# Every fourth late expert row of the prompt is weighted and summed by GpSimd instead of VectorE

## The chip, the cores and the metric

The kernel runs on one core of a Trainium2 chip. The metric is the device time of one execution in microseconds. Three runs of the kernel before took 5117.41, 5132.25 and 5138.71 us; their median, 5132.25 us, is the time before.

## The reference

One inference step of a two-layer backbone over 128 prompt tokens and 512 latent tokens, D = 1024, all in float32. Each layer has four token mixers whose results are merged through gates, an output projection, and then an expert layer. Only the expert layer matters here:

```python
def chunk(hc):                                     # 128 tokens
    qry = (hc @ w_query).reshape(-1, PEER_HEADS, 2, PEER_DK // 2)
    s = jnp.einsum('thpk,hpnk->thpn', qry, sub_keys)
    s1, i1 = lax.top_k(s[:, :, 0], PEER_TOPK)
    s2, i2 = lax.top_k(s[:, :, 1], PEER_TOPK)
    cand = (s1[..., :, None] + s2[..., None, :]).reshape(-1, PEER_HEADS, PEER_TOPK * PEER_TOPK)
    sc, ci = lax.top_k(cand, PEER_TOPK)
    e = ...                                        # 8 heads x 16 experts for each token
    g = jax.nn.softmax(sc, axis=-1)
    act = jax.nn.gelu(jnp.einsum('thkd,td->thk', u_tab[e], hc), approximate=False)
    return jnp.einsum('thk,thkd->td', g * act, v_tab[e])
```

So each token has 128 experts, and each expert a row of 2048 numbers (u, then v): the dot product of u with the token's vector gives a weight, and the result is the weighted sum of the 128 rows v. The 128 prompt tokens lie on the 128 partitions, so "row i" below is the i-th expert of every prompt token at once: 128 x 8 KB, 1 MB.

## The kernel before

The program has five instruction streams written out by hand (SyncE, GpSimd, ScalarE, VectorE, TensorE) that are tied by semaphores. Nothing reorders them: each engine runs its stream in the order of the code.

SyncE streams the weights in chunks of 512 KB through a ring of six (`wring`). GpSimd gathers the expert rows with indirect DMAs. For the prompt that are 128 rows in each layer (`PAIRS`). The first 16 (`EARLY`) are gathered while the latent tokens' queries and keys are made (L630). The other 112 are gathered (L664) during the latent tokens' merge (32 steps), output projection (8 steps) and expert query (16 steps): three rows in each merge step, one in each output step, one in each of the first eight query steps. They go into a ring of four slots, `prow`, with `NP = 4`.

What is done with row i, engine by engine:

- GpSimd waits on `p_acc` until row i-4 has been added, which frees its slot, and issues the gather of row i (L664).
- VectorE waits for the row (`p_row`), forms its dot product (`prompt_dot`, L1397) and then adds the row *before* it, i-1, to the sum `yacc` (`prompt_add`, L1407), when its weight is there.
- ScalarE makes the weight from the dot product: Gelu (L844), then times the gate (L845), counted on `p_w`.

`prompt_rows` gives VectorE's order: dot(i), add(i-1), dot(i+1), add(i), and so on. In a merge step it stands behind the evacuation of the gate product (L1633) and the addition to the merged sum (L1636). TensorE's merge step has 8 products against the gate's weights (L2129) and 4 against the branch's (L2134), each recorded as two matmuls, and may be two steps ahead of L1633. ScalarE makes the step's sigmoid (L1006), then the weights of that step's rows.

After the last add (row 127, in query step 8) VectorE routes the first latent tokens (L1137 to L1200); then GpSimd begins the 512 gathers of the latent tokens (L681). Before the second of these it waits for the prompt's last add, and so does TensorE before it turns `yacc`. In layer 0 and 1 all of this is the same.

Of the kernel before, what the change touches and what calls it, by code (L numbers as in the profile page):

```python
# [9 lines left out]
ALU = mybir.AluOpType  # L10
# [5 lines left out]
D = 1024  # L16
# [19 lines left out]
PAIRS = HEADS * TOPK  # L36
# [197 lines left out]
NP = 4  # L234
EARLY = 16
# [15 lines left out]
    return range(120 + n, 121 + n) if n < 8 else ()  # L251


class Chain:

    def __init__(self, eng, sem):
# [15 lines left out]
def need(eng, s, n):  # L272

    if n > 0:
        eng.wait_ge(s, n)


def backbone(nc, xT, cT, w, ada, small, rowg, lamrow, clay, poolw, subk, rope, edge, mask, bias, ckn, ckd,
             cvn, cvd, experts, y_prompt, y_sample, o_nk, o_nv, o_dk, o_dv):
    with ExitStack() as cx:  # L280
# [3 lines left out]
        def sem(name):  # L284
            return cx.enter_context(nc.semaphore(name))
# [6 lines left out]
        arena = sb("arena", [P, 28800])  # L292
# [24 lines left out]
        def at(tensor, start, *shape):  # L317
            n = int(np.prod(shape))
            v = tensor[:, start:start + n]
            if len(shape) == 1:  # L320
                return v
            names = "abcd"[:len(shape)]
            return v.rearrange(f"p ({' '.join(names)}) -> p {' '.join(names)}", **dict(zip(names, shape)))
# [68 lines left out]

        prow = [at(arena, a, 2 * D) for a in (16512, 18560, 10368, 14464)]
        prow0 = [at(arena, a, 2 * D) for a in (20096, 22144, 24704)]
        yacc0, yacc = at(arena, 27392, D), at(arena, 22656, D)
        pdots, pgel, pwcol = at(T, 2048, PAIRS), at(T, 2176, PAIRS), at(T, 2304, PAIRS)

        w_load = [sem(f"w_load{i}") for i in range(RING)]
# [15 lines left out]
        p_idx, p_top, p_gexp, p_gok = sem("p_idx"), sem("p_top"), sem("p_gexp"), sem("p_gok")  # L414
        p_row = [sem(f"p_row{i}") for i in range(NP)]
        p_row0 = [sem(f"p_row0{i}") for i in range(3)]
        p_dot, p_w, p_acc = sem("p_dot"), sem("p_w"), sem("p_acc")

        x_ready, sq_ready, root, h_ready = sem("x_ready"), sem("sq_ready"), sem("root"), sem("h_ready")
        sq_half = sem("sq_half")  # L420
# [56 lines left out]
        def row_of(i):  # L477
            return prow0[i % 3] if i < EARLY else prow[i % NP]

        def weight_of(i):  # L480
            return stp[:, i:i + 1] if i < EARLY else pwcol[:, i:i + 1]
# [4 lines left out]
        def pause(eng):  # L486

            eng.nop(nofuse=True)
# [34 lines left out]
        def _(gp):  # L523
            own = Chain(gp, pool_own)
# [76 lines left out]
            for l in range(DEPTH):  # L601
# [23 lines left out]
                gp.wait_ge(p_idx, 2 * l + 1)  # L625
                for i in range(EARLY):
                    if i >= 3:
                        gp.wait_ge(p_acc, l * PAIRS + i - 2)
                    pause(gp)
                    gp.indirect_dma_start(row_of(i), None, experts,  # L630
                                          bass.IndirectOffsetOnAxis(ap=peidx[:, i:i + 1], axis=0)).then_inc(p_row0[i % 3], 16)
                gp.wait_ge(p_acc, l * PAIRS + EARLY)
                pause(gp)
                vg = vscr.rearrange("(r c) n -> r c n", c=GRID_W)
                for j in range(NJ):
# [17 lines left out]

                gp.wait_ge(o_ready, NJOBS * (l + 1))
                gp.wait_ge(p_idx, 2 * (l + 1))
                for i in range(EARLY, PAIRS):
                    if i >= EARLY + NP:
                        gp.wait_ge(p_acc, l * PAIRS + i - NP + 1)
                    if i == EARLY + 3:
                        gp.wait_ge(y_diff, 4 * (l + 1))  # L660
                    if i == EARLY + 8:
                        pause(gp)
                        gp.dma_start(sk, subk[l]).then_inc(subk_in, 16)
                    gp.indirect_dma_start(row_of(i), None, experts,  # L664
                                          bass.IndirectOffsetOnAxis(ap=peidx[:, i:i + 1], axis=0)).then_inc(p_row[i % NP], 16)

                mixer = prompt_mixer(l + 1) if l + 1 < DEPTH else iter(())
                step = None
                for t in range(NL):
                    for i in range(PAIRS):  # L670
                        n = (l * NL + t) * PAIRS + i
                        here = t * PAIRS + i
                        if i % GP == 0:
                            gp.wait_ge(idx_ready, (l * NL + t) * 2 + i // GP + 1)
                        if here == 1:
                            gp.wait_ge(p_acc, PAIRS * (l + 1))
                        if here == 7:
                            wait_unit(gp, ("E", l, "ynP"))
                        if n >= NS:
                            gp.wait_ge(v_done, n - NS + 1)  # L680
                        gp.indirect_dma_start(rows[:, n % NS, :], None, experts,  # L681
                                              bass.IndirectOffsetOnAxis(ap=eidx[:, t % 2, i:i + 1], axis=0)).then_inc(row_in[n % NS], 16)
                        if here == PAIRS:
                            wait_unit(gp, ("C", l, "s15"))
                            step = next(mixer, None)
                        elif step is not None and here >= gather_of(step) + 10:
                            step = next(mixer, None)
# [423 lines left out]
        def _(v):  # L1111
            own = Chain(v, dve_own)
# [260 lines left out]
            def prompt_route(l):  # L1373

                for k in range(12, 16):
                    wait_freed(v, ("P", l, f"s{k}"))
                for g in range(2):
                    yield from route(l, proute, pscores[:, 8 * g:8 * g + 8, :], peidx[:, GP * g:GP * (g + 1)], pgate[:, GP * g:GP * (g + 1)],
                                     p_idx, p_top, lambda: need(v, p_acc, l * PAIRS))

            def prompt_soften(l):

# [16 lines left out]
            def prompt_add(l, i):  # L1399

                v.wait_ge(p_w, l * PAIRS + i + 1)
                row = row_of(i)[:, D:2 * D]
                if i == 0:
                    v.tensor_scalar(yacc0, row, weight_of(i), None, ALU.mult).then_inc(p_acc, 1)
                else:
                    v.wait_ge(p_acc, l * PAIRS + i)
                    v.scalar_tensor_tensor(yacc0 if i < EARLY else yacc, row, weight_of(i), yacc0 if i <= EARLY else yacc, ALU.mult, ALU.add).then_inc(p_acc, 1)  # L1407

            def prompt_rows(l, which):

                for i in which:
                    prompt_dot(l, i)
                    if i not in (0, EARLY):
                        prompt_add(l, i - 1)

            mixer = prompt_mixer(0)
# [8 lines left out]
            for l in range(DEPTH):  # L1425
# [285 lines left out]
                for n in range(17):  # L1711
                    if n < 16:
                        prompt_rows(l, prompt_rows_at("query", n))
                    if n >= 1:
                        take_scores("L", 0, n - 1)
                    if n == 8:
                        prompt_add(l, PAIRS - 1)
                        for k in range(4, 8):
                            wait_freed(v, u(f"s{k}"))
                        first = latent_route(0, 0)  # L1720
                    if first:
                        for _ in range(10):
                            next(first, None)
# [43 lines left out]
        def _(pe):  # L1767
# [195 lines left out]
            for l in range(DEPTH):  # L1963
# [228 lines left out]

                for t in range(2):
                    turn_norm(t)
                pe.wait_ge(p_acc, PAIRS * (l + 1))
                turned(("E", l, "ynP"), [yacc[:, k * P:(k + 1) * P] for k in range(KD)])

                def turn_experts(t):
# [146 lines left out]
```

## Time and profile before

| | |
|---|---|
| three runs | 5117.41, 5132.25, 5138.71 us |
| the profiled execution | 5121.45 us |
| its span, first to last instruction | 5119.6 us |
| granted TensorE clock, mean | 0.966 |
| merge, output and query stage with the late prompt rows, layer 0 | 861.9 to 1343.7 us |
| the same, layer 1 | 3307 to 3787 us |

The profile is one execution. Busy time is the time in which an engine works on its instructions; GpSimd's time for a gather is that of issuing it, not of the transfer. Idle time is put down to what ended it. "Issue to landing" runs from the start of the issuing instruction until the data has arrived.

### The profile page before, as it was taken

What the parts mean: (1) busy time and instruction counts of PE and PEld (TensorE: products, weight loads), DVE (VectorE), ACT (ScalarE), POOL (GpSimd) and SP (SyncE); (2) the same over time, 40 slices, a digit from 0 to 9 for tenths busy, and PEclk for the clock granted to TensorE, in tenths of its full rate; (3) what the DMA queues carried; (4) which work ended last, traced back from release to release, by engine and by line L of the source; (5) the groups of instructions that cost most, each with busy time, mean ns of one, the idle gap of its engine ahead of it and who ended that gap; (6) DMA issues with size and microseconds to landing.
All of it is one profiled execution on the core that took longest, in us unless ns stands there. A gap on an engine that the chain in (4) does not pass through costs nothing.

```text
span 5119.6 us, 46892 instructions
## 1 busy us (share of the span) xinstructions
PE 4417.8 (86%) x14388; PEld 2284.2 (45%) x14388; DVE 3388.3 (66%) x7266; ACT 1951.3 (38%) x5074; POOL 1661.8 (32%) x1600
## 2 busy tenths in 40 slices
PE   7889888998899888888888898999889987777777
PEld 4674455434645333344544444644464632222222
DVE  4239865777787677775444896777778767576544
ACT  1210543343233434565533035544323433333333
POOL 3003121223244453433332322132224444434332
PEclk8899989999999999999999998999999999999999
DMA  7752526999799999999999143199979999999998
GB/s 286 252 192 79 191 78 249 350 345 351 305 420 420 420 420 411 413 394 418 405 419 419 60 140 124 61 356 356 360 279 420 412 419 422 422 421 419 421 421 353
DMA packets 277115, 1677.27 MB, mean 328 GB/s; under 512 B 31808, under 2 KB 31856, under 8 KB 112384
## 3 DMA queue, kind: packets, MB, share of 16 engines
q0 software_dynamic: 190896, 1365.43, 66.0%
q1 hardware_dynamic: 82944, 302.03, 16.1%
q10 hardware_dynamic: 3024, 6.82, 0.3%
q8 instruction: 115, 1.88, 0.1%
q14 instruction: 136, 1.11, 0.1%
HBM read 1667.33 MB, written 6.82 MB: 327 GB/s over the span
## 4 chain that ended last, share of the span: by engine, by line
DMA 39%; PE 31%; DVE 17%; ACT 7%; issue 5%; POOL 0%; SPq 0%; DVEq 0%; ACTq 0%; POOLq 0%
DMA arena<-experts,bsb 27%; PE ps L2218 12%; DMA arena<-experts,peidx 10%; PE ps L1805 5%; DVE arena L1496 4%; DVE arena L1708 3%; PE ps L1913 2%; PE ps L1980 2%; DMA wring<-w 2%; DVE arena L1407 2%; PE ps L2070 2%; PE ps L2092 2%; PE ps L1781 1%; ACT L1066 1%; ACT T L1070 1%
## 5 line engine op out<-in xcount | busy, mean ns | idle before, releaser
L2218 PE MATMUL ps<-arena,T 128*128 128x512 f32 x4096 | 1967.6, 614 | 445.2 <-ACT T L1070 444.6
L1708 DVE CUSTOM_DVE_ANT_0 arena<-arena,h_sb 128x1024 f32<-128x1024 f32 x1024 | 1252.8, 1227 | 865.0 <-DMA arena<-experts,bsb 861.4
L681 POOL DMA_INDIRECT arena<-experts,bsb x1024 | 1095.8, 1070 | 1741.4 <-PE ps L2218 1582.2
L2218 PEld LDWEIGHTS ps<-arena,T 128*128 128x128 f32 x4096 | 726.1, 192 | 1569.5 <-ACT T L1070 951.7
L1066 ACT ACTIVATE bsb<-T 128x1 f32<-128x1 f32 x1024 | 205.9, 201 | 1303.0 <-DVE T L1708 1301.3
L1805 PE MATMUL ps<-h_sb,wring 128*128 128x256 f32 (+2 forms) x2304 | 517.8, 382 | 35.1 <-DVE h_sb L1447 13.7
L2129 PE MATMUL ps<-h_sb,wring 128*128 128x512 f32 x1024 | 457.6, 600 | 33.5 <-DVE arena L1633 31.0
L1805 PEld LDWEIGHTS ps<-h_sb,wring 128*128 128x128 f32 x2304 | 380.7, 196 | 183.8 <-issue 152.0
L664 POOL DMA_INDIRECT arena<-experts,peidx x224 | 249.5, 1114 | 655.6 <-DVE arena L1407 582.1
L1070 ACT ACTIVATE T<-ident,bsb 128x128 f32<-128x128 f32 x1024 | 410.9, 401 | 33.5
L1397 DVE CUSTOM_DVE_ANT_0 arena<-arena,h_sb 128x1024 f32<-128x1024 f32 x256 | 312.7, 1222 | 113.7 <-DMA arena<-experts,peidx 112.6
L1980 PE MATMUL ps<-wring,h_sb 128*128 128x512 f32 x768 | 338.2, 598 | 0.0
L2129 PEld LDWEIGHTS ps<-h_sb,wring 128*128 128x128 f32 x1024 | 192.6, 191 | 294.3 <-issue 228.1
L1067 ACT ACTIVATE bsb<-bsb,T 128x1 f32<-128x1 f32 x1024 | 301.4, 294 | 33.2
L1407 DVE SCALAR_TENSOR_TENSOR arena<-arena,T 128x1024 f32<-128x1024 f32 x224 | 287.0, 1281 | 0.5 <-ACT T L845 0.5
L2134 PE MATMUL ps<-arena,wring 128*128 128x512 f32 x512 | 230.2, 593 | 0.0
L1980 PEld LDWEIGHTS ps<-wring,h_sb 128*128 128x128 f32 x768 | 146.2, 193 | 175.3 <-issue 175.3
L844 ACT ACTIVATE T<-T 128x1 f32<-128x1 f32 x224 | 45.3, 202 | 444.0 <-DVE T L1397 444.0
L1496 DVE SCALAR_TENSOR_TENSOR arena<-arena,sm 128x512 f32<-128x512 f32 x240 | 184.9, 849 | 0.0
L1805 PE MATMUL ps<-arena,wring 128*128 128x256 f32 (+1 forms) x768 | 150.4, 353 | 25.8 <-DVEq L1639 25.0
L2070 PE MATMUL ps<-arena 64*128 64x128 f32 (+2 forms) x512 | 151.8, 433 | 17.3 <-ACT T L961 15.2
L630 POOL DMA_INDIRECT arena<-experts,peidx x32 | 64.9, 2029 | 284.4 <-DVE arena L1407 171.6
(326 smaller groups left out, 4543.1 us busy)
## 6 DMA issues: line engine op xcount, KB each, us to landing
wring<-w SPq DMA_DIRECT2D x576, 512.0 KB, 6.2
arena<-experts,bsb POOLq DMA_INDIRECT x1024, 15.3
bsb<-bias POOLq DMA_DIRECT2D x16, 512.0 KB, 3.8
arena<-subk POOLq DMA_DIRECT2D x4, 1024.0 KB, 8.3
arena<-experts,peidx POOLq DMA_INDIRECT x256, 8.0
arena<-v_scratch POOLq DMA_DIRECT2D x64, 64.0 KB, 2.0
x_sb<-xT POOLq DMA_DIRECT2D x1, 2048.0 KB, 14.1
v_scratch<-arena ACTq DMA_DIRECT2D x8, 256.0 KB, 2.0
```

Source lines behind the costliest of these rows:

```text
L681: gp.indirect_dma_start(rows[:, n % NS, :], None, experts, bass.IndirectOffsetOnAxis(ap=eidx[:, t % 2, i:i + 1], axis=0)).then_inc(row_in[ ...
L1066: own.link(act.activation(gel[:, i:i + 1], dots[:, t % 2, i:i + 1], ACT.Gelu))
L1067: own.link(act.activation(wcol[:, i:i + 1], gel[:, i:i + 1], ACT.Copy, scale=gate[:, t % 2, i:i + 1]))
L1070: act.activation(diag[:, n % ND, :], ident[:], ACT.Copy, scale=wcol[:, i:i + 1]).then_inc(diag_ok, 1)
L1397: v.tensor_tensor_reduce(e, e, htok(NL), 1.0, 0.0, ALU.mult, ALU.add, d).then_inc(p_dot, 1)
L1407: v.scalar_tensor_tensor(yacc0 if i < EARLY else yacc, row, weight_of(i), yacc0 if i <= EARLY else yacc, ALU.mult, ALU.add).then_inc(p_acc, 1)
L1496: op = v.scalar_tensor_tensor(acc[:, c, :], U[:, c, 1 + k:1 + k + LAT], S(col), acc[:, c, :], ALU.mult, ALU.add)
L1708: v.tensor_tensor_reduce(e, e, htok(t), 1.0, 0.0, ALU.mult, ALU.add, dots[:, t % 2, i:i + 1]).then_inc(dot, 1)
L1805: mm = pe.matmul(bank(key, cols), chunk_of(s, l, c)[:, k * P:(k + 1) * P], src(k), start=(k == 0), stop=(k == KD - 1))
L1980: mm = pe.matmul(bank(key), h_sb[:, t, k, :], chunk_of("L", l, c0 + q)[:, kk * 512:(kk + 1) * 512], start=(k == 0), stop=(k == KD - 1))
L2129: mm = pe.matmul(ps[:, s % 2, :], chunk_of("L", l, c)[:, k * P:(k + 1) * P], h_in(k), start=(k == 0), stop=(k == KD - 1))
L2218: mm = pe.matmul(ps[:, 6 + half, :], diag[:, n % ND, :], rows[:, n % NS, D + half * 512:D + (half + 1) * 512], start=(i == 0), stop=(i == ...
```

## The change

Of the rows from 16 on, those with i % 4 == 2 (18, 22, ..., 126; 28 of 112) are no longer added by VectorE. GpSimd sums them into a second accumulator `yaccg`. It does so in its own stream, just before the gather that reuses the slot: wait for the row's weight, multiply the row in place by its weight, add it to `yaccg`, wait for its own completion, then issue the gather. For row 18 the multiply writes `yaccg` directly. After the loop it sums row 126. VectorE, after adding row 127, adds `yaccg` to `yacc`. Since `p_acc` now counts only what VectorE adds, `added(l, i)` gives the counts to wait for, 101 in a layer instead of 128.

```diff
+def pool_row(i):
+    return i >= EARLY and i % NP == 2
+
+POOL_ROWS = sum(pool_row(i) for i in range(PAIRS))
+ADDED = PAIRS - POOL_ROWS + 1
+
+def added(l, i):
+    return l * ADDED + sum(not pool_row(j) for j in range(i + 1))
...
-        yacc0, yacc = at(arena, 27392, D), at(arena, 22656, D)
+        yacc0, yacc, yaccg = at(arena, 27392, D), at(arena, 22656, D), at(arena, 23680, D)
...
@@ gpsimd
+                def prompt_sum(i):
+                    k = l * POOL_ROWS + (i - EARLY) // NP
+                    gp.wait_ge(p_w, l * PAIRS + i + 1)
+                    pause(gp)
+                    row = row_of(i)[:, D:2 * D]
+                    if i < EARLY + NP:
+                        gp.tensor_scalar(yaccg, row, weight_of(i), None, ALU.mult).then_inc(p_accg, 1)
+                    else:
+                        own.link(gp.tensor_scalar(row, row, weight_of(i), None, ALU.mult))
+                        gp.tensor_tensor(yaccg, yaccg, row, ALU.add).then_inc(p_accg, 1)
+                    gp.wait_ge(p_accg, k + 1)
+                    pause(gp)
+
                 for i in range(EARLY, PAIRS):
                     if i >= EARLY + NP:
-                        gp.wait_ge(p_acc, l * PAIRS + i - NP + 1)
+                        if pool_row(i - NP):
+                            prompt_sum(i - NP)
+                        else:
+                            gp.wait_ge(p_acc, added(l, i - NP))
...
+                prompt_sum(PAIRS - 2)
...
                         if here == 1:
-                            gp.wait_ge(p_acc, PAIRS * (l + 1))
+                            gp.wait_ge(p_acc, ADDED * (l + 1))
...
@@ vector
-                                     p_idx, p_top, lambda: need(v, p_acc, l * PAIRS))
+                                     p_idx, p_top, lambda: need(v, p_w, l * PAIRS))
...
             def prompt_rows(l, which):
                 for i in which:
                     prompt_dot(l, i)
-                    if i not in (0, EARLY):
+                    if i not in (0, EARLY) and not pool_row(i - 1):
                         prompt_add(l, i - 1)
...
                         prompt_add(l, PAIRS - 1)
+                        v.wait_ge(p_accg, POOL_ROWS * (l + 1))
+                        v.wait_ge(p_acc, added(l, PAIRS - 1))
+                        v.tensor_tensor(yacc, yacc, yaccg, ALU.add).then_inc(p_acc, 1)
...
@@ tensor
-                pe.wait_ge(p_acc, PAIRS * (l + 1))
+                pe.wait_ge(p_acc, ADDED * (l + 1))
```

GpSimd's stream in the prompt's late gathers of layer 0 before: all 112 gathers (L664) stand together, parted only by the load of `subk` (L663).

```order
L664 DMA arena<-experts,peidx 128x2048 x8
L663 DMA arena<-subk 128x2048
L664 DMA arena<-experts,peidx 128x2048 x104
L681 DMA arena<-experts,bsb 128x2048 x129
```

The same place now (L697 is the gather, L696 the load of `subk`, L679 and L681 the multiply, L682 the addition to `yaccg`):

```order
L697 DMA arena<-experts,peidx 128x2048 x6
L679 TENSOR_SCALAR arena<-arena,T 128x1024
L697 DMA arena<-experts,peidx 128x2048 x2
L696 DMA arena<-subk 128x2048
L697 DMA arena<-experts,peidx 128x2048 x2
L681 TENSOR_SCALAR arena<-arena,T 128x1024
L682 TENSOR_TENSOR arena<-arena 128x1024
L697 DMA arena<-experts,peidx 128x2048 x4
L681 TENSOR_SCALAR arena<-arena,T 128x1024
L682 TENSOR_TENSOR arena<-arena 128x1024
L697 DMA arena<-experts,peidx 128x2048 x4
```

The last four rows repeat. A multiply and an addition now stand between every fourth gather and the one behind it.

VectorE's stream in a merge step before (L1633 the evacuation, L1397 a dot product and the read of its sum, L1407 the add of the row before):

```order
L1633 TENSOR_TENSOR arena<-ps,arena 128x2x256
L1397 ISA arena,T<-arena,h_sb 128x1024
L1397 ISA T 128x1
L1407 SCALAR_TENSOR_TENSOR arena<-arena,T 128x1024
L1397 ISA arena,T<-arena,h_sb 128x1024
L1397 ISA T 128x1
L1407 SCALAR_TENSOR_TENSOR arena<-arena,T 128x1024
L1397 ISA arena,T<-arena,h_sb 128x1024
L1397 ISA T 128x1
L1407 SCALAR_TENSOR_TENSOR arena<-arena,T 128x1024
```

The same step now (L1667 is L1633, L1431 is L1397, L1441 is L1407):

```order
L1667 TENSOR_TENSOR arena<-ps,arena 128x2x256
L1431 ISA arena,T<-arena,h_sb 128x1024
L1431 ISA T 128x1
L1431 ISA arena,T<-arena,h_sb 128x1024
L1431 ISA T 128x1
L1441 SCALAR_TENSOR_TENSOR arena<-arena,T 128x1024
L1431 ISA arena,T<-arena,h_sb 128x1024
L1431 ISA T 128x1
L1441 SCALAR_TENSOR_TENSOR arena<-arena,T 128x1024
```

Here the add behind the first dot product, that of GpSimd's row, is gone. Every fourth add is gone so; everything else keeps its order.

## Rows read from the trace of the kernel before

**Rows 1.** The page's totals: engine, busy us, share of the span, instructions.

```profile
PE 4417.8 (86%) x14388; PEld 2284.2 (45%) x14388; DVE 3388.3 (66%) x7266; ACT 1951.3 (38%) x5074; POOL 1661.8 (32%) x1600
```

**Rows 2.** Chain of waits, 862 to 1330 us: shares by line, then start us, us, what.

```profile
by line: DMA arena<-experts,peidx 57.0%; issue 10.7%; PE ps L1805 10.0%; DVE arena L1407 8.8%; PE ps L2129 4.5%; PE ps L2134 2.2%; PE ps L2159 1.1%; DVE T L1397 0.6%; ACT L1006 0.5%; DVE arena L1397 0.5%; DVE T L1439 0.4%; DVE bsb L1166 0.4
861.88 7.11 PE ps L2129 x16
...
872.42 6.87 PE ps L2129 x16
...
1069.19 1.21 DVE arena L1407
1070.66 7.95 DMA arena<-experts,peidx
```

**Rows 3.** Merge stretches: length; PE, PEld, DVE, ACT, POOL busy; clock; DMA share; GB/s.

```profile
950.00:1030.00 80.00, 71.50 (x163) 30.41 (x162) 57.64 (x75) 32.80 (x62) 22.18 (x20) 1.00 0.92 347
1030.00:1110.00 80.00, 78.36 (x177) 33.54 (x176) 60.75 (x79) 33.64 (x65) 23.63 (x22) 0.98 0.93 351
```

**Rows 4.** Waits from 862 to 1330 us: total us, times, longest.

```profile
POOL arena L664 <- DVE arena L1407: 291.3, 107, 9.8
DVE arena L1397 <- DMA arena<-experts,peidx: 59.4, 55, 4.4
PEld ps L2129 <- DVE arena L1633: 37.2, 24, 4.0
```

**Rows 5.** The gathers L664 from 860 to 1300 us.

```profile
L664 POOL DMA_INDIRECT arena<-experts,peidx x109: 932/936/1953, 878.1 to 1293.5; - x109
DMA to landing us min/median/max: 5.5/8.2/11.0
```

**Rows 6.** Timeline of VectorE, then of ScalarE, in one merge step.

```profile
1067.96 1.23 DVE L1397 CUSTOM_DVE_ANT_0 arena<-arena,h_sb 128x1024 f32<-128x1024 f32 x1 [1.16 <-DMA arena<-experts,peidx]
1069.11 1.28 DVE L1407 SCALAR_TENSOR_TENSOR arena<-arena,T 128x1024 f32<-128x1024 f32 x1
1071.79 0.69 DVE L1633 TENSOR_TENSOR arena<-ps,arena 128x512 f32<-128x512 f32 x1 [1.40 <-ACT arena L1006]
...
1069.22 0.20 ACT L844 ACTIVATE T<-T 128x1 f32<-128x1 f32 x1 [3.06 <-DVE T L1397]
1069.46 0.30 ACT L845 ACTIVATE T<-T,pgate 128x1 f32<-128x1 f32 x1
```

**Rows 7.** GpSimd's own operations, by line and in the timeline.

```profile
L604 POOL TENSOR_TENSOR arena<-x_sb x8: 1882/1890/1912, 100.2 to 2833.1; 128x1024 f32<-128x1024 f32 x8
L560 POOL TENSOR_SCALAR arena<-arena x8: 527/664/932, 83.6 to 1883.3; 128x128 f32<-128x128 f32 x8
L560 POOL TENSOR_SCALAR bsb<-bsb x8: 1502/1734/1737, 425.6 to 2944.9; 128x512 f32<-128x512 f32 x8
...
85.48 0.29 POOL L588 COPY arena<-arena 128x128 f32<-128x128 f32 x1 [0.19 <-POOL arena L592]
...
423.58 0.61 POOL L617 COPY bsb<-arena 128x512 f32<-128x512 f32 x1 [52.60 <-ACT arena L870]
424.34 1.08 POOL L549 TENSOR_TENSOR bsb<-bsb 128x543 f32<-128x543 f32 x1 [0.15 <-POOL bsb L617]
```

**Rows 8.** VectorE and GpSimd at the same time: the convolution; later a dot product.

```profile
429.63 35.49 DVE L1496 SCALAR_TENSOR_TENSOR arena<-arena,sm 128x512 f32<-128x512 f32 x34
464.38 15.98 DVE L1496 SCALAR_TENSOR_TENSOR arena<-arena,sm 128x512 f32<-128x512 f32 x24
L1496 DVE SCALAR_TENSOR_TENSOR arena<-arena,sm x20: 737/1092/1780, 429.6 to 449.8; 128x512 f32<-128x512 f32 x20
...
1715.04 1.90 POOL L579 TENSOR_TENSOR arena<-x_sb 128x1024 f32<-128x1024 f32 x1
...
1714.51 3.52 DVE L1708 CUSTOM_DVE_ANT_0 arena<-arena,h_sb 128x1024 f32<-128x1024 f32 x1 [0.86 <-DMA arena<-experts,bsb]
```

**Rows 9.** GpSimd's first gather for the latent tokens in layer 0.

```profile
1343.74 0.94 POOL L681 DMA_INDIRECT arena<-experts,bsb  x1 [49.31 <-DVE bsb L1200]
```

More of the change, by code:

```diff
@@ L416, in backbone @@
         p_row0 = [sem(f"p_row0{i}") for i in range(3)]
-        p_dot, p_w, p_acc = sem("p_dot"), sem("p_w"), sem("p_acc")
+        p_dot, p_w, p_acc, p_accg = sem("p_dot"), sem("p_w"), sem("p_acc"), sem("p_accg")
         x_ready, sq_ready, root, h_ready = sem("x_ready"), sem("sq_ready"), sem("root"), sem("h_ready")
@@ L627, in _ @@
                     if i >= 3:
-                        gp.wait_ge(p_acc, l * PAIRS + i - 2)
+                        gp.wait_ge(p_acc, added(l, i - 3))
                     pause(gp)
@@ L631, in _ @@
                                           bass.IndirectOffsetOnAxis(ap=peidx[:, i:i + 1], axis=0)).then_inc(p_row0[i % 3], 16)
-                gp.wait_ge(p_acc, l * PAIRS + EARLY)
+                gp.wait_ge(p_acc, added(l, EARLY - 1))
                 pause(gp)
@@ L1405, in prompt_add @@
                 else:
-                    v.wait_ge(p_acc, l * PAIRS + i)
+                    v.wait_ge(p_acc, added(l, i - 1))
                     v.scalar_tensor_tensor(yacc0 if i < EARLY else yacc, row, weight_of(i), yacc0 if i <= EARLY else yacc, ALU.mult, ALU.add).then_inc(p_acc, 1)
```

## The prediction

> **What bounds the kernel now.** I began with the page's own totals. No engine fills the span: TensorE is busy 86% of it, VectorE 66%, GpSimd 32% [rows 1]. So what the change is worth has to be read in its own stage, the merge, output and query steps of the latent tokens, in which the 112 late prompt rows are gathered. In layer 0 that stage runs from 861.9 us to the first latent gather at 1343.7 us [rows 2, 9]; layer 1 repeats it.
>
> The chain of waits over that stage is the view that decides: 57% of it is a prompt row in flight from DRAM, 8.8% the VectorE add L1407, and TensorE's matmuls have only the smaller part [rows 2]. The reader should see there a regular alternation: a row's transfer of some 8 us, then the add of 1.21, then the next transfer. The stretches of 80 us say the same from the engines' side [rows 3]: TensorE is busy 72 to 79 of 80, VectorE 58 to 61, the DMA engines 0.92, but nothing is at its limit all the time.
>
> The waits name the loop [rows 4]. GpSimd stands idle 291 us in this stage of layer 0 until an add L1407 is done; VectorE stands idle 59 us until a row has landed; TensorE waits for the evacuation L1633, which is queued on VectorE behind those rows. In the code a slot of the four-row ring is free only when the row's add is done, and that add stands on VectorE behind the dot product of the *next* row. So one turn of the loop is: GpSimd issues row j+3, it lands, its dot product, the add of row j+2, the issue of row j+6. From the rows [rows 5, 6]: issue to landing 8.2 (median), dot product 1.14 from its start to the add's start, add 1.28, 0.27 from its end (1070.39) to the next issue (1070.66 [rows 2]): 10.9 us for three rows, 14.5 for four. Measured are 108 intervals of issues in 1293.5 - 878.1 = 415.4 us [rows 5], 3.85 us each, 15.4 us for four rows. The loop explains nearly all of the pace; the rest are turns in which VectorE waits for a gate (1.40 us in the timeline [rows 6]).
>
> **The change, part by part.** Counted from the code, for each layer: 28 rows (18, 22, ..., 126) leave VectorE. 28 scalar_tensor_tensor of 1.28 go, and one tensor_tensor of 128x1024 comes ahead of the latent routing (about 1.23). GpSimd gets 28 tensor_scalar and 27 tensor_tensor of 128x1024, in line with its own gathers.
>
> *What VectorE saves.* 1.28 us in four rows. VectorE is busy 60 us of 80 [rows 3], about 11.5 of the 15.4 us of four rows, and idles for the rest. By itself this gives nothing unless the freed 1.28 stood on the loop; on GpSimd's path it is replaced by something longer.
>
> *What GpSimd pays.* A tensor_tensor of this very size takes 1.89 [rows 7]. The tensor_scalar has no row of this size: the multiply by a constant on 512 elements takes at least 1.50 and on 128 at least 0.53 [rows 7], which is 2.54 ns for each further element, so 0.53 + 896 x 2.54 ns = 2.80 us. Between dependent GpSimd instructions lie 0.15 us [rows 7].
>
> *The shared read.* When GpSimd's pooling runs beside VectorE's convolution, both stretch. Thirty-four scalar_tensor_tensor take 35.49 us, where 24 of them without company take 15.98, 0.67 each [rows 8]; GpSimd's 512-element multiply goes from 1.50 to a median of 1.73 [rows 7]. One dot product, 1.23 otherwise [rows 6], takes 3.52 around a GpSimd tensor_tensor of 1.90 [rows 8]. I give each GpSimd operation 0.3 us of waiting. The dot product, scalar_tensor_tensor and tensor_tensor that fill this stage on VectorE all read two tensors of SBUF, so this will be met here. This is the rule of the Trainium skill, page "SBUF — State Buffer", section "Who interferes with whom": a VectorE instruction with two SBUF inputs and a GpSimd instruction that reads SBUF exclude each other, and the second waits for the whole first one. By that rule, the trace agrees, with the 3.52.
>
> On VectorE's side a pair can cost up to 3.52 - 1.23 = 2.3 us for the tensor_tensor and, from L1496's median of 1.09 against its least of 0.74 [rows 8], 0.35 on 512 elements, perhaps 0.7 for the multiply. That is 3.0 against 1.28 saved, so VectorE's load *rises* by up to 1.7 us in four rows, to 13.2 of 15.4. It stays covered by VectorE's idle time.
>
> *The new turn.* Let row p be one of GpSimd's. When VectorE has added row p-1, GpSimd issues row p+3 (0.27 + 0.94). Its weight is long there (two short instructions of ScalarE after the dot product, 0.20 and 0.30 [rows 6]). Then it multiplies (0.15 + 2.80 + 0.30), adds (0.15 + 1.89 + 0.30), goes on (0.15) and only now issues row p+4: 6.95 us after the add of p-1. Before, that issue waited for the add of row p, which could be done some 2.4 us (1.14 + 1.28) after the add of p-1. Row p+4 lands, its dot product takes 1.14, and behind it stands the add of row p+3 (1.28), which corresponds to the add of p-1: the turn of four rows is closed. Queued on GpSimd behind the pair are the gathers of p+4 and p+5, whose slots may already be free; on VectorE the dot products of those rows wait, behind them the evacuation L1633, and TensorE for that.
>
> The landing is the unknown. The median is 8.2 us with 0.92 of the DMA engines busy; the fastest landing took 5.5 [rows 5]. Row p+4 goes out after a pause of 5.7 us in which no row was issued, so it meets a link with less in it than the median row. I take 7.0, near the middle. The turn is then 6.95 + 7.0 + 1.14 + 1.28 = 16.4 us against 15.4: 1.0 us more. At 5.5 it would be 14.9, under the present pace, and no loss; at 8.2 it is 17.6, 2.2 more.
>
> *The sum.* 26 such turns in a layer (rows 22 to 122; row 18 has one operation and 126 no gather behind it) by two layers by 1.0 us = 52 us. The added tensor_tensor stands ahead of the routing on which the first latent gather waits, so it is fully on the path: 2 x 1.23 with its hand-over, 3 us. The routing's wait, moved from the adds to the weights, and the changed semaphore targets cost nothing: they are met long before. The latent expert stage behind it keeps its instructions. The profiled execution took 5121.45 us; 5121.45 + 55 = 5176. It lies 10.8 us under the median of the three runs (5132.25), from which the same sum gives 5187. I predict 5182.
>
> **The rivals.**
>
> *B, a cheap multiply: no change.* If GpSimd multiplies by a column at the pace at which it copies (0.29 for 128 elements, 0.61 for 512 [rows 7], so 0.61 + 512 x 0.83 ns = 1.04 us), the turn is 14.6 us at a landing of 7.0, below today's 15.4. The pair then hides in GpSimd's idle 291 us, and other turns of the loop set the pace as now: 5121.45 + 3 = 5125 us. Against it stands that the row of the tensor_scalar itself is three times as steep as that of the copy. For it, that this row multiplies by a constant and the new one by a column, which no row shows. The Trainium skill's page "GPSIMD Engine Reference", section "Engine selection", speaks for B: operations with one input run at roughly one element per cycle on GpSimd. By it the time would be B's, by the tensor_scalar's row the forecast's; the trace agrees for the copy, not for the tensor_scalar.
>
> *C, VectorE's relief counts: faster.* Place: TensorE waits for the evacuation L1633, 24 times and 37.2 us in this stage of layer 0 [rows 4]. In three steps of four an add of 1.20 would be gone from ahead of it: 24 x 3/4 x 1.2 = 21.6 us a layer, 43 in both, less the 3: 5081 us. It decides only if the GpSimd turn falls well below the present one, that is if the two operations with their gaps take under about 4 us, and if GpSimd's reads don't hold VectorE up, which rows 8 speak against. TensorE's own work of a step (872.42 - 861.88 = 10.5 us in the first, which waits for nothing [rows 2]) and the DMA engines at 0.92 leave little room below 11.
>
> *D, the slow end.* The landing stays at 8.2 because VectorE's dot products, stretched by the shared read, are late too: 52 x 2.2 + 3 = 117, 5239 us.
>
> **How the numbers follow.** The forecast has 0.60, B 0.24, C 0.06, D 0.10. A difference of 0.5%, 26 us on the median of 5132, is about what a measurement of this kernel can tell from none. The forecast and D lie above 5158, which gives slower 0.70; B, with a little of C, is "same", 0.25; the rest of C is faster, 0.05. The range takes in B's 5125 and ends at D's 5239: 5123 to 5240. What is left out is C and the tail above D. The forecast's own range is 5160 to 5220.
>
> **What would show it.** In the profile after: GpSimd's tensor_scalar of 128x1024 at 2.8 to 3.1 us and its tensor_tensor at 1.9 to 2.2, once in four gathers; four issues of rows in 16.4 us instead of 15.4; more idle time of VectorE until a row has landed, above 59 us a layer; dot products of more than 1.23 us where GpSimd reads; the first latent gather about 27 us later in each layer, and everything behind it as long as before. I am wrong if the multiply takes about 1 us (B), if rows issued behind the pair land in 5.5 us and the pace stays at 15.4, or if TensorE's waits for L1633 shrink.

## The result, and the profile after

The changed kernel takes 5221.24 us (median of 4 runs, 5216.61 to 5225.03) against 5135.14 for the kernel before: the ratio is 1.0177, 95% interval 1.0159 to 1.0194. It is 86 us slower. The forecast was 5182, with 5123 to 5240 as the range; the direction was right, and the size was underestimated: the sum had 55 us. The narrower range given for the forecast's own mechanism, 5160 to 5220, is missed by 1 us, and the time lies nearer to rival D's 5239 than to 5182.

The page's totals after, as in [rows 1]: span; then busy us, share and instructions of each engine.

```profile
span 5223.2 us, 47006 instructions
PE 4452.4 (85%) x14388; PEld 2295.9 (44%) x14388; DVE 3410.5 (65%) x7212; ACT 1952.7 (37%) x5074; POOL 2010.0 (38%) x1710
```

VectorE has 54 instructions fewer and is busy 22 us *longer*. GpSimd is busy 348 us more. The span has grown by 103.6 us from one profiled execution to the other; the medians differ by 86, since the execution profiled before was one of the quick ones (5121.45) and the one after, 5225.03, wasn't.

Where the time went: GpSimd's first latent gather of layer 0, the end of the stage [rows 9].

```profile
1396.24 1.01 POOL L715 DMA_INDIRECT arena<-experts,bsb  x1 [34.71 <-DVE bsb L1234]
```

It is 52.5 us later than before, where the prediction had about 27, and layer 1 repeats it: its first latent gather comes at 3890.3 instead of 3787.3, 103.0 later. From there to the last gather layer 1 takes 1302.7 us, before 1303.0: the rest has not changed.

The new operations (name: least, median, most ns):

```profile
L681 POOL TENSOR_SCALAR arena<-arena,T x54: 2859/2860/3742, 906.7 to 3848.7; 128x1024 f32<-128x1024 f32 x54
L682 POOL TENSOR_TENSOR arena<-arena x54: 2337/2347/3420, 909.6 to 3852.0; 128x1024 f32<-128x1024 f32 x54
```

The multiply is where its own row of before put it (2.80 and 0.3), not where the copy's row would have (1.04): rival B is gone. The addition takes at least 2.34, not the 1.89 of [rows 7]. That row multiplies a tensor by itself, the new one adds two tensors; which of the two differences counts, no run shows.

Waits from 862 to 1375 us, as in [rows 4]:

```profile
POOL arena L697 <- DVE arena L1441: 149.9, 61, 7.3
DVE arena L1431 <- DMA arena<-experts,peidx: 92.0, 49, 5.3
PEld ps L2166 <- DVE arena L1667: 57.2, 17, 5.5
...
POOL arena L697 <- POOL arena L682: 20.5, 26, 0.9
```

GpSimd waits less for adds (149.9 instead of 291.3), since it works in that time. VectorE waits more for rows (92.0 instead of 59.4), and TensorE more for the evacuation (57.2 instead of 37.2). The last row is new: after each pair GpSimd stands still for 0.79 us before the gather. (Pair beside, below, shows that 0.5 of it is the `pause` of the kernel.)

Two stretches of the merge, as in [rows 3]:

```profile
950.00:1030.00 80.00, 69.69 (x157) 29.70 (x156) 55.13 (x63) 31.39 (x57) 50.56 (x30) 0.98 0.87 326
1030.00:1110.00 80.00, 69.35 (x150) 29.64 (x149) 53.05 (x63) 28.97 (x56) 47.91 (x28) 0.94 0.81 295
```

The DMA engines are less busy (0.81 to 0.87, before 0.92 to 0.93): there are holes in the stream of rows. TensorE is less busy too, and its granted clock is lower, 0.98 and 0.94 after 1.00 and 0.98 in the same stretches. Its products against the gate's weights take 626 ns in the mean of both layers instead of 600. Whether this slower clock is part of the cause is taken up with the turn, below.

One turn of the ring, first GpSimd, then VectorE (start us, us, what, idle before and its releaser):

```profile
1073.93 1.79 POOL L697 DMA_INDIRECT arena<-experts,peidx  x1 [0.66 <-DVE arena L1441]
1075.76 2.86 POOL L681 TENSOR_SCALAR arena<-arena,T 128x1024 f32<-128x1024 f32 x1
1078.70 2.83 POOL L682 TENSOR_TENSOR arena<-arena 128x1024 f32<-128x1024 f32 x1
1082.31 1.19 POOL L697 DMA_INDIRECT arena<-experts,peidx  x1 [0.78 <-POOL arena L682]
1083.80 1.99 POOL L697 DMA_INDIRECT arena<-experts,peidx  x1 [0.30 <-issue]
...
1092.99 0.94 POOL L697 DMA_INDIRECT arena<-experts,peidx  x1 [5.95 <-DVE arena L1441]
...
1078.11 1.22 DVE L1431 CUSTOM_DVE_ANT_0 arena<-arena,h_sb 128x1024 f32<-128x1024 f32 x1
1079.25 3.37 DVE L1441 SCALAR_TENSOR_TENSOR arena<-arena,T 128x1024 f32<-128x1024 f32 x1
1082.54 1.21 DVE L1431 CUSTOM_DVE_ANT_0 arena<-arena,h_sb 128x1024 f32<-128x1024 f32 x1
...
1090.29 1.23 DVE L1431 CUSTOM_DVE_ANT_0 arena<-arena,h_sb 128x1024 f32<-128x1024 f32 x1 [5.33 <-DMA arena<-experts,peidx]
1091.44 1.28 DVE L1441 SCALAR_TENSOR_TENSOR arena<-arena,T 128x1024 f32<-128x1024 f32 x1
```

Follow the loop: issue of row p+3 at 1073.93; pair; issue of p+4 at 1082.31; its dot product at 1090.29, for which VectorE had waited 5.33 us; the add of p+3 behind it at 1091.44; the issue of p+7 at 1092.99. This turn took 19.1 us, 2 more than the mean. Beside it stands the second effect: the add at 1079.25 lasts 3.37 instead of 1.28. It begins while GpSimd's addition runs (1078.70 to 1081.53) and ends 1.1 us behind it. The gathers behind the pair take 1.19 and 1.99 to issue instead of 0.94.

### The profile page after: what moved, and what is told of

Read it like the earlier page. It is cut to its first block, busy times and chain, and to the rows that moved or that the text cites. A ratio compares the mean times of both kernels' runs of the same rounds, so it can differ in the third digit from the quotient of the medians.

```text
span 5223.2 us, 47006 instructions
## 1 busy us (share of the span) xinstructions
PE 4452.4 (85%) x14388; PEld 2295.9 (44%) x14388; DVE 3410.5 (65%) x7212; ACT 1952.7 (37%) x5074; POOL 2010.0 (38%) x1710
## 4 chain that ended last, share of the span: by engine, by line
DMA 35%; PE 30%; DVE 17%; ACT 8%; issue 7%; POOL 4%; SPq 0%; DVEq 0%; ACTq 0%; POOLq 0%
DMA arena<-experts,bsb 26%; PE ps L2255 12%; DMA arena<-experts,peidx 6%; PE ps L1842 5%; DVE arena L1530 4%; DVE arena L1742 3%; PE ps L1950 2%; PE ps L2017 2%; DMA wring<-w 2%; PE ps L2107 2%; PE ps L2129 2%; POOL arena L697 2%; DVE arena L1441 1%; ACT L1100 1%; ACT T L1104 1%
## 5 line engine op out<-in xcount | busy, mean ns | idle before, releaser
L1742 DVE CUSTOM_DVE_ANT_0 arena<-arena,h_sb 128x1024 f32<-128x1024 f32 x1024 | 1252.9, 1227 | 867.4 <-DMA arena<-experts,bsb 860.9
L715 POOL DMA_INDIRECT arena<-experts,bsb x1024 | 1112.8, 1087 | 1696.1 <-PE ps L2255 1567.8
L2166 PE MATMUL ps<-h_sb,wring 128*128 128x512 f32 x1024 | 482.0, 626 | 90.9 <-DVE arena L1667 86.7
L1431 DVE CUSTOM_DVE_ANT_0 arena<-arena,h_sb 128x1024 f32<-128x1024 f32 x256 | 359.2, 1405 | 176.3 <-DMA arena<-experts,peidx 175.1
L697 POOL DMA_INDIRECT arena<-experts,peidx x224 | 276.3, 1233 | 437.5 <-DVE arena L1441 305.9
L1441 DVE SCALAR_TENSOR_TENSOR arena<-arena,T 128x1024 f32<-128x1024 f32 x168 | 250.4, 1491 | 1.4 <-ACT T L879 1.3
L645 POOL DMA_INDIRECT arena<-experts,peidx x32 | 65.0, 2033 | 284.5 <-DVE arena L1441 171.8
```

Source lines behind the costliest of these rows:

```text
L697: gp.indirect_dma_start(row_of(i), None, experts, bass.IndirectOffsetOnAxis(ap=peidx[:, i:i + 1], axis=0)).then_inc(p_row[i % NP], 16)
L715: gp.indirect_dma_start(rows[:, n % NS, :], None, experts, bass.IndirectOffsetOnAxis(ap=eidx[:, t % 2, i:i + 1], axis=0)).then_inc(row_in[ ...
L1431: v.tensor_tensor_reduce(e, e, htok(NL), 1.0, 0.0, ALU.mult, ALU.add, d).then_inc(p_dot, 1)
L1742: v.tensor_tensor_reduce(e, e, htok(t), 1.0, 0.0, ALU.mult, ALU.add, dots[:, t % 2, i:i + 1]).then_inc(dot, 1)
L2166: mm = pe.matmul(ps[:, s % 2, :], chunk_of("L", l, c)[:, k * P:(k + 1) * P], h_in(k), start=(k == 0), stop=(k == KD - 1))
```

## The experiments

Two theories. Theory 1: GpSimd's operations stand in line before a gather, inside the loop that frees a slot of the ring, and what counts is their time. Theory 2: what counts is that they read SBUF together with VectorE, whose instructions become longer. The table gives all runs; "merge step" is the distance of layer 0's 32 evacuations (the last start less the first, by 31), read from the evacuation's line in each trace.

| kernel | us | ratio to before (95%) | merge step, us |
|---|---|---|---|
| before | 5129 to 5135 | 1 | 11.27 |
| changed | 5221.2 | 1.0177 (1.0159 to 1.0194) | 12.63 |
| changed, once more | 5219.7 | 1.0176 (1.0155 to 1.0196) | 12.59 |
| nothing in line | 5120.5 | 0.9980 (0.9968 to 0.9992) | 11.16 |
| memsets in line | 5201.5 | 1.0133 (1.0112 to 1.0153) | 12.35 |
| multiply only | 5153.7 | 1.0038 (1.0019 to 1.0056) | 11.49 |
| pair beside, VectorE adds all | 5234.6 | 1.0203 (1.0179 to 1.0226) | 12.60 |
| every eighth row | 5167.4 | 1.0066 (1.0045 to 1.0088) | 11.74 |
| before, five slots | 5055.2 | 0.9850 (0.9827 to 0.9873) | 10.13 |
| changed, five slots | 5111.4 | 0.9962 (0.9947 to 0.9977) | 10.98 |
| five slots, memsets in line | 5101.8 | 0.9947 (0.9933 to 0.9961) | 10.79 |
| five slots, nothing in line | 5051.1 | 0.9852 (0.9826 to 0.9878) | 10.13 |
| before, five slots, once more | 5056.7 | 0.9859 (0.9834 to 0.9885) | 10.13 |

**Nothing in line.** The relief without the price. (Here and in the other kernels that leave rows out, the counts of `p_accg` go with the edit.)

```diff
-                        own.link(gp.tensor_scalar(row, row, weight_of(i), None, ALU.mult))
-                        gp.tensor_tensor(yaccg, yaccg, row, ALU.add).then_inc(p_accg, 1)
+                        pass
```

> The changed kernel, but GpSimd only waits for the weight of its rows 22 to 126 and neither multiplies nor adds them, and VectorE doesn't either: those rows are left out of the sum. It is VectorE's relief without its price. Theory 1 (GpSimd's operations stand in the loop that frees a ring slot): with nothing in line the turn of four rows is at most the old one, so the time is 5132 or less; if the relief counts, as rival C had it, down to 5080. Theory 2 (the shared read of SBUF makes VectorE's and the gathers' instructions longer): the same. A time of 5132 +- 15 means that the relief of VectorE is worth nothing, whatever GpSimd does.

It took 5120.5: 0.2% less than before, within the 5132 +- 15 that was to mean no worth. VectorE is rid of 28 adds of 1.28 us in each layer and has one addition of 1.23 more, 69 us of work less in both layers, and that is worth some 10 us (4 to 16 by the interval). VectorE was not the bound, and rival C's 5081 isn't reached even where GpSimd pays nothing.

**Memsets in line.** The same place and nearly the same time, but nothing is read.

```diff
-                        own.link(gp.tensor_scalar(row, row, weight_of(i), None, ALU.mult))
-                        gp.tensor_tensor(yaccg, yaccg, row, ALU.add).then_inc(p_accg, 1)
+                        for _ in range(3):
+                            own.link(gp.memset(at(arena, 8320, 2 * D), 0.0))
```

> The changed kernel, but GpSimd does three memsets of 128x2048 of a spare region where the multiply and the add stood; the rows 22 to 126 of GpSimd are left out of the sum. The memsets should take about 1.8 us each, 5.8 in line with the gaps, somewhat less than the pair (about 6.5), and read no SBUF. Theory 1: most of the loss stays, 5180 to 5215. Theory 2: the loss goes, the time is within 20 us of that of the kernel with nothing in line.

It took 5201.5, ratio 1.0133. First two of its places in line (timeline of GpSimd), then VectorE's dot products and adds in this kernel, and last the same two rows of the changed one (least/median/most ns):

```profile
1061.57 5.55 POOL L682 MEMSET arena<- 128x2048 f32 x3
1067.92 1.46 POOL L697 DMA_INDIRECT arena<-experts,peidx  x1 [0.80 <-POOL arena L682]
...
1077.82 5.55 POOL L682 MEMSET arena<- 128x2048 f32 x3
1084.16 0.94 POOL L697 DMA_INDIRECT arena<-experts,peidx  x1 [0.80 <-POOL arena L682]
```

```profile
L1431 DVE CUSTOM_DVE_ANT_0 arena<-arena,h_sb x108: 1209/1225/1451, 901.4 to 1347.2; 128x1024 f32<-128x1024 f32 x108
L1441 DVE SCALAR_TENSOR_TENSOR arena<-arena,T x80: 1274/1280/1284, 903.7 to 1344.4; 128x1024 f32<-128x1024 f32 x80
```

```profile
L1431 DVE CUSTOM_DVE_ANT_0 arena<-arena,h_sb x110: 1210/1224/3369, 882.2 to 1346.9; 128x1024 f32<-128x1024 f32 x110
L1441 DVE SCALAR_TENSOR_TENSOR arena<-arena,T x82: 1273/1280/3368, 884.5 to 1348.0; 128x1024 f32<-128x1024 f32 x82
```

From the first memset to the gather are 6.35 us (1067.92 - 1061.57); in the changed kernel from the multiply to the gather 6.42 in the mean of 25 places. VectorE is hardly touched: its adds take 1.284 us at the most and its dot products 1.451, where the changed kernel has 3.368 and 3.369. And yet 72 us of loss are there. (The profiled execution, 5220.7, is not typical: the three others took 5200.8 to 5201.7, and its first evacuation comes at 900.8, that of the changed kernel at 881.6. The merge step in the table begins behind that delay.) So the time in line makes three quarters to four fifths of the loss; the changed kernel's remaining 15 to 20 us (1.0177 against 1.0133) are left for the shared read, less what the two kernels differ in line. Theory 2 expected a time near 5120 and is refuted as the main cause. That a memset leaves VectorE alone is also what the Trainium skill says, page "SBUF — State Buffer", section "Who interferes with whom": a VectorE instruction with two SBUF inputs excludes only GpSimd instructions that read; these runs agree, 1.284 against 3.368.

**Multiply only.** (The rows of GpSimd from 22 on are multiplied and not added.)

```diff
-                        own.link(gp.tensor_scalar(row, row, weight_of(i), None, ALU.mult))
-                        gp.tensor_tensor(yaccg, yaccg, row, ALU.add).then_inc(p_accg, 1)
+                        own.link(gp.tensor_scalar(row, row, weight_of(i), None, ALU.mult))
```

> The changed kernel with the multiply but without the add to the second sum (rows 22 to 126 of GpSimd left out of it). In line are 3.2 us instead of 6.5. Theory 1: there is a threshold, since the turn before had room beside other waits: 16.9 - 3.3 = 13.6 us, under the 15.1 of before, so the time is 5135 or less. Theory 2: the multiply holds the shared read for only about a quarter of the pair's time, so 5155 or less. If costs add up in proportion to GpSimd's busy time it is 5175.

5153.7, ratio 1.0038 (1.0019 to 1.0056). Theory 1's threshold is missed by 19 us, theory 2's bound of 5155 is just met, and 5175, in proportion to busy time, isn't reached. By itself this run doesn't part the theories; the memsets do. In line are 3.7 us from the multiply to the gather, not 3.2, against 6.4 with the pair. There is a bend, since more than half of the pair's time costs a quarter of its loss, but no sharp threshold. The table of turns in the part on the prediction shows why: the time from issue to dot product gets shorter while the time in line grows.

**Pair beside.** The kernel before with the pair on spare data.

```diff
+                    if i >= EARLY + NP and (i - NP) % NP == 2:
+                        gp.wait_ge(p_w, l * PAIRS + i - NP + 1)
+                        pause(gp)
+                        spare = at(arena, 8320, 2, D)
+                        own.link(gp.tensor_scalar(spare[:, 0], spare[:, 0], weight_of(i - NP), None, ALU.mult))
+                        own.link(gp.tensor_tensor(spare[:, 1], spare[:, 1], spare[:, 0], ALU.add))
                     if i >= EARLY + NP:
                         gp.wait_ge(p_acc, l * PAIRS + i - NP + 1)
```

> The kernel before, in which GpSimd does a multiply and an add of 128x1024 on a spare region at the places of the changed kernel, after the weight of the same rows; VectorE adds all rows, nothing is left out. It has the whole price and no relief. If VectorE's relief is worth nothing in the changed kernel, this takes the same, 5221 +- 20. If the relief is worth its 1.28 us in each turn (52 x 1.28 = 67), it takes 5290.

5234.6, ratio 1.0203: 13 to 15 us above the changed kernel, though the intervals of the two overlap (1.0179 to 1.0226, 1.0159 to 1.0194). VectorE's relief is not worth 67 us; that it is worth anything beside GpSimd's work is not clear of the noise. Nor is the comparison exact, since this kernel has no last addition on VectorE and, by its edit, no `pause` (a no-op in GpSimd's stream) between the pair and the gather. The trace shows what that is worth:

```profile
1078.84 2.63 POOL L662 TENSOR_TENSOR arena<-arena 128x1024 f32<-128x1024 f32 x1
1081.74 1.69 POOL L670 DMA_INDIRECT arena<-experts,peidx  x1 [0.27 <-POOL arena L662]
```

From the end of the addition to the gather are 0.27 us, where the changed kernel, with a `pause` in that place, has 0.78. The kernel before shows the same 0.5 us: from the end of VectorE's add to the gather are 0.77 us in 24 of 24 places at L630, which has a `pause`, and 0.27 in 190 of 216 at L664, which has none.

**Every eighth row.**

```diff
-    return i >= EARLY and i % NP == 2
+    return i >= EARLY and i % 8 == 2
```

> The changed kernel in which GpSimd sums every eighth late row (18, 26, ..., 122) instead of every fourth; nothing is left out. Each pair delays the turn in which it stands. If each of them costs the same by itself, the loss is half: 5132 + 43 = 5175. If the ring catches up in the turn that has no pair, it is less than half: 5140 to 5160.

5167.4, ratio 1.0066 (1.0045 to 1.0088): between the two expectations, 37% of the loss for half of the pairs, with half (1.0088) just at the edge of the interval. Whether the ring catches up in the turns without a pair is not settled by it.

**Five slots.** If the loop is the cause, a longer ring must help both kernels. 2048 elements of the arena are free in this stage.

```diff
-NP = 4
+NP = 5
...
-        prow = [at(arena, a, 2 * D) for a in (16512, 18560, 10368, 14464)]
+        prow = [at(arena, a, 2 * D) for a in (16512, 18560, 10368, 8320, 14464)]
...
-            return prow0[i % 3] if i < EARLY else prow[i % NP]
+            return prow0[i % 3] if i < EARLY else prow[(i - EARLY) % NP]
...
-                    if i == EARLY + 3:
+                    if i == EARLY + 4:
...
-                        if here == 1:
+                        if here == 0:
```

(The counts of `p_row` go with it.)

> The kernel before with a fifth slot in the ring of the late prompt rows (2048 elements of the arena that are free in this stage); nothing is left out. Theory 1 says that the loop of the slots sets the pace before: with a fifth slot four rows instead of three are in one turn of 10.9 us, 2.7 us a row, and the pace is then set by the weights and rows on the link or by TensorE, 10.4 to 10.8 us a merge step instead of 11.3: 64 x 0.7 = 45 us less, 5090, between 5070 and 5110. If the loop isn't the bound, 5132.

5055.2 and, again, 5056.7: 1.4 to 1.5% faster than before, beyond the 5070 to 5110 that was expected. Two stretches of its merge:

```profile
950.00:1030.00 80.00, 80.00 (x188) 35.48 (x187) 67.05 (x89) 38.05 (x73) 33.27 (x25) 1.00 0.99 394
1030.00:1110.00 80.00, 80.00 (x187) 35.34 (x186) 64.20 (x84) 37.70 (x72) 29.84 (x24) 1.00 0.98 383
```

TensorE is busy 80 of 80 us and the DMA engines 0.98 to 0.99: the merge step is at 10.1 us, in which TensorE is never idle, and the loop is out of the way. This is the version that beats both.

> The changed kernel with the same fifth slot; nothing is left out, GpSimd sums the same rows as in the changed kernel. Theory 1: the fifth slot covers the 6.5 us in line, most of the 86 us of loss goes: 5110 to 5150, and at most 40 above the kernel before with five slots. Theory 2: VectorE and the gathers are held by GpSimd's reads as before, so at least 60 us above the kernel before with five slots.

5111.4: better than the changed kernel by 110 us, better even than before, but 56 us above its own companion with five slots. That is more than the 40 that theory 1 allowed and less than the 60 that theory 2 asked for.

**Five slots, memsets or nothing in line.** To settle those 56 us:

```diff
-                        own.link(gp.tensor_scalar(row, row, weight_of(i), None, ALU.mult))
-                        gp.tensor_tensor(yaccg, yaccg, row, ALU.add).then_inc(p_accg, 1)
+                        for _ in range(6):
+                            own.link(gp.memset(yaccg, 0.0))
```

(In this one the last addition on VectorE adds `yacc` to itself instead of `yaccg`.)

> The changed kernel with five slots, in which GpSimd does six memsets of 128x1024 (about 1.0 us each with the gap, 6.1 in line) instead of the pair; GpSimd's rows from 22 on are left out of the sum. It asks what the 56 us are that the pair still costs with five slots (5111 against 5055). If it is GpSimd's own time (four gathers and the pair take 13 to 14 of the 14.9 us of a turn, and GpSimd idles only a quarter of its former time), most stays: 5085 to 5110. If it is the shared read, which held VectorE up by 1 to 2 us in each pair, it goes: 5055 to 5070. With reads gone the gathers' issue should also return from about 1.3 to 1.1 us.

> The changed kernel with five slots and nothing in line on GpSimd; its rows from 22 on are left out of the sum. TensorE was busy 80 of 80 us in the merge with five slots, so VectorE's relief can't show: 5055 +- 10, as the kernel before with five slots.

5101.8 with memsets, 5051.1 with nothing in line. Of the 56 us, some 45 to 50 stay when nothing is read. Two stretches of the kernel with memsets, to be held against those above:

```profile
950.00:1030.00 80.00, 79.97 (x187) 35.13 (x186) 54.81 (x75) 34.42 (x68) 63.19 (x58) 1.00 0.93 359
1030.00:1110.00 80.00, 76.25 (x175) 32.59 (x175) 54.26 (x74) 36.26 (x66) 57.38 (x56) 1.00 0.94 367
```

GpSimd is busy 57 to 63 of 80 us instead of 30 to 33, and the gaps around each of its instructions come on top. It is GpSimd's time again. Whether it acts there through the turn of five slots or because GpSimd is nearly full itself was not told apart. The issue of a gather, expected to return from 1.3 to 1.1 us, came to 1.18 in the mean of layer 0; but the kernel before with five slots, which has no pair at all, has 1.31.

The changed kernel was also run a second time:

> The changed kernel again, beside the others on the same chip: 5221 +- 8.

5219.7. The same was done with the faster kernel:

> The kernel before with five slots once more, beside the two above: 5055 +- 8.

5056.7.

## Why the prediction was right, and where its size was off

**The bound was named rightly.** That a loop through the four slots sets the pace, not an engine, is shown by the fifth slot: without changing any work it takes 1.5% off, and TensorE, busy 72 to 78 of 80 us before [rows 3], is busy for all 80.

**The relief of VectorE.** I gave it nothing; it is worth some 10 us of the 69 removed where nothing stands in line.

**The new turn, term by term.** From the start times in the trace, the mean over 24 turns of layer 0 (rows 22 to 114), against the working of the prediction:

| term | predicted | before | changed |
|---|---|---|---|
| issue of p+3 to issue of p+4 | 6.68 | 3.43 | 7.58 |
| issue of p+4 to its dot product | 7.0 | 8.98 | 6.80 |
| dot product to the add behind it | 1.14 | 1.15 | 1.15 |
| add | 1.28 | 1.28 | 1.28 |
| its end to the issue of p+7 | 0.27 | 0.30 | 0.30 |
| turn | 16.4 | 15.1 | 17.1 |

The turn of four rows, the step on which the sum rested, closes as described. The landing, the term for which I had the widest bounds (5.5 to 8.2), came out nearly right: 6.56 us in the mean and 0.25 more until VectorE began the dot product, 6.8 for 7.0. It is also what softens the blow: 4.15 us more between the issues cost only 2.0 us of turn, because the dot product of row p+4 begins 2.2 us sooner after its issue. Of that the landing has 1.8 (8.35 before) and VectorE 0.4 (0.63 before).

The same two terms in the other kernels with four slots, the same 24 turns:

| kernel | issue of p+3 to issue of p+4 | issue of p+4 to its dot product | turn |
|---|---|---|---|
| nothing in line | 1.59 | 10.68 | 15.0 |
| before | 3.43 | 8.98 | 15.1 |
| multiply only | 5.01 | 7.75 | 15.5 |
| memsets in line | 7.47 | 6.54 | 16.7 |
| changed | 7.58 | 6.80 | 17.1 |

The sooner row p+4 is issued behind row p+3, the longer it takes until its dot product. With nothing in line VectorE stood waiting for the row in 11 of the 24 turns, and it came 10.2 us after its issue in these. From 1.59 to 3.43 us the second term gives back nearly all that the first takes, up to 5.01 three quarters, and up to 7.58 little more than a third; the fastest landing of any row is 5.5 us before and 5.4 in the changed kernel. That is the bend between multiply only, 11.49 us a step, and the pair, 12.63, and with nothing in line it is why issuing the row 1.8 us sooner shortens the turn by only 0.1.

The turns also answer for TensorE's lower clock. VectorE's evacuation waits for TensorE, and could so hold up the dot product of a landed row; but between landing and dot product lie 0.25 us, less than the 0.63 before. So the lower clock adds nothing to the turns counted here. It is seen where TensorE waits longer; no run held the clock fixed.

Two terms were mis-sized. Of the 1.0 us by which a turn's loss was underestimated, the new turn has 0.7 and the old one 0.3:

- *The time in line.* 6.42 us from the multiply to the gather where I had 5.59 (2.80 + 0.30 + 0.15 + 1.89 + 0.30 + 0.15). The addition takes 2.34 or more, 2.65 in the mean of layer 0; and from its end to the gather are 0.79 us, where I had put the 0.15 that lies between two arithmetic instructions. Half a microsecond of that is the kernel's own `pause`, which the code shows and the sum left out; at the 0.6 us of turn that each further microsecond costs between multiply only and the pair, it is worth some 16 us in 52 turns, an estimate that no run tested. The gather in front of the pair can be longer too, 1.79 in the turn shown instead of 0.94, beside a dot product.
- *The turn before.* I set the new turn against 15.4 us, the mean of all gathers, in which the slower output and query steps are contained. The turns to which the working applies took 15.1. The loss of a turn is 2.0, not 1.0; by 52 turns it is 104 us, and the span grew by 103.6. (That agreement is luck: the medians differ by 86, and the output and query steps lose less in a turn than the merge. The merge alone, 32 steps in each layer, grew by 88 us.)

**The shared read.** It was predicted as covered by VectorE's idle time, with up to 1.7 us more load in four rows. A single add is stretched as far as was given (3.37; 3.52 was the bound from [rows 8]), but VectorE's load rose by 22 us in 52 turns, 0.4 us a turn. Covered it is mostly: the kernels with memsets, which lack it, are 0.4% and 0.2% faster, 20 and 10 us, at a similar time in line; for five slots the intervals overlap, so those 10 us may be noise. In one point the reading of [rows 8] went too far: there the dot product begins 0.53 us before GpSimd's instruction and is yet the one that is stretched, so the row shows that the two exclude each other, but its recorded starts don't show that the later one waits.

**Rival D.** It gave 5239 with a landing that stays at 8.2 us, and the time came within 18 us of it. But the landing fell to 6.6; the time is where it is by the time in line, not by D.

**Added addition of 1.23 on the path.** As predicted, 1.225; it was not tried alone.

## What to carry to other kernels

An engine that stands idle for most of a stage may be idle *inside* a loop; work put into its queue ahead of the instruction that closes the loop lengthens the turn by all that the transfer in that loop doesn't give back, here 2.0 of 4.15 us. Count what stands between the instructions as well: the `pause` behind the pair took 0.5 us. Before moving work off an engine, ask what the move is worth if the work simply vanished: here 10 us of 69, which one run shows. When a ring's turn (issue, landing, use, release) divided by its slots is near the pace, try one more slot before balancing engines: it took 72 to 77 us off here, and the same move of work then cost 56 us instead of 86 to 88.

## What the runs showed of the hardware that was not expected

- GpSimd's tensor_scalar with a column as factor takes 2.86 us on 128x1024 float32, its tensor_tensor that adds two different tensors 2.34, while a memset of 128x2048 takes 1.81: arithmetic on one input is the slowest of the three for each element.
- From the end of a GpSimd arithmetic instruction to the start of the indirect DMA that waits for it are 0.27 us (pair beside), and 0.78 with a no-op between them (changed kernel); from gather to gather are 0.30, from one memset to the next under 0.1.
- A row issued longer after the one ahead of it is there sooner: with 1.6 us between the two issues its dot product comes 10.7 us after its issue, with 7.6 us between them 6.8.
- Issuing a gather takes 0.94 us, but up to 2.0 beside VectorE's dot products and adds (in the kernel before, none of the 118 late gathers that ran clear of them took over 1.02); in the changed kernel 1.25 in the mean of layer 0 instead of 1.13.
